# Bias rows of the gates as a pair of float32r rows instead of one float32 row, in a two-layer block on one core

## The chip, the cores and the metric

The kernel runs on one core of a Trainium2 chip. The metric is the device time of one execution in microseconds (us). Three executions of the kernel before took 2523.35, 2525.79 and 2533.22 us; their median is 2525.79 us.

## The reference

The program is a hybrid attention layer on 256 tokens of width 2048, followed by a recurrent layer with a convolutional feed-forward part. The change touches one product of the first layer, the projection that makes the gates:

```python
proj = jnp.einsum('bsd,dc->bsc', hn, w_in)                # hn: 256 x 2048
gates = jax.nn.sigmoid(proj[..., QKVG_COLS + N_HEADS:] + b_gate).reshape(b, s, N_BRANCH, D_MODEL)
# each branch's output is multiplied by its gate, and the three are summed
merged = sum over n of gates[:, :, n] * (y[n] @ w_up[n])  # 256 x 2048
```

`b_gate` has 3 x 2048 entries. The kernel treats it as twelve pieces of 512, one for each block of 512 gate columns.

## The kernel before

**Products.** Every large product takes its weights through four slots of 2 x 512 columns. For each such unit SyncE (SP) loads `w_raw`, ScalarE (ACT) writes its rounded part `w_hi` in float32r (L502), VectorE (DVE) writes the remainder `w_lo` (L839), and TensorE (PE) runs twelve matmuls (L1408): two chunks, two token tiles, and three terms (hi x hi, hi x lo, lo x hi). The semaphores `hi_done`, `lo_done` and `used` count units. ACT and DVE run two units ahead of PE; SP runs four ahead of DVE. The order on each engine is written out by hand, and each engine works strictly down its own list.

**Gate blocks.** Blocks 12 to 15 (`seg == 3`) are the gates of branch 0: eight units each, in alternating PSUM banks. ACT evacuates each with a sigmoid into `xn` (L581). Four short products with `w_up` follow; DVE multiplies each by its gate into `merged` (L1012).

**Pairs.** Then a hardware loop of four rounds, each with two halves (`j`), goes through eight pairs: a gate product of eight units in PSUM bank 0, and an up product of two units in bank 1. ACT turns the gate into `sg` by a sigmoid (L590). When the up product is done, DVE multiplies it by `sg` (L1021) and adds it to `merged` (L1023). PE does not wait for these two: its next gate product needs bank 0 alone, and that has been evacuated (`evac_act`). After the second half of a round DVE also copies a row of another product, the modulation (`mod_copy`, L957). Modulation units (L1435, two matmuls of 32 output rows) are woven between the units of the large products: `every_other`.

**Bias.** The bias enters PSUM ahead of a gate product, as a matmul with one row: `add_row` multiplies a one-row constant of ones by `brow`, once for each token tile.

```python
def add_row(bank):                                             # L1421 to L1423
    for rt in range(RT):
        pe.matmul(gemm_ps[:, bank, rt], C("sel", 1, 0, P), brow[:, :], start=True, stop=False)
```

SP fetches `brow` (L370, L380) when the gate product before has used the old one, and PE waits for that load (`brow_in`).

Of the kernel before, what the change touches and what calls it, by code (L numbers as in the profile page):

```python
# [4 lines left out]
F32 = mybir.dt.float32  # L22
F32R = mybir.dt.float32r
# [6 lines left out]
P = 128  # L30
T = 256
RT = T // P
D = 2048
# [132 lines left out]
def build(nc, a):  # L166
    base = (nc.sbuf_base + 31) // 32 * 32

    def at(name, shape, dtype, kb):
        return nc.alloc_sbuf_tensor_at(name, shape, dtype, offset=base + int(kb * KB))  # L170
# [15 lines left out]
    br = [at(f"br{i}", [P, RT, 4 * BW], F32, 129.5 + 16 * i) for i in range(2)]  # L186
    ys_hi = at("ys_hi", [P, NBR * HEADS, T], F32R, 161.5)
    ys_lo = at("ys_lo", [P, NBR * HEADS, T], F32R, 173.5)
    brow = at("brow", [1, NBLK], F32, 185.5)
    relb = at("relb", [P, HEADS, T], F32, 189.5)  # L190
    tmpT = at("tmpT", [P, 2, UK, T], F32, 193.5)
    sg = at("sg", [P, RT, NBLK], F32, 193.5)
# [91 lines left out]
    def S(name):  # L284
        if name not in sems:
            sems[name] = nc.alloc_semaphore(name)
        return sems[name]

    raw_in = [S(f"raw_in{i}") for i in range(SLOTS)]
    brow_in = S("brow_in")  # L290
    mod_in = [S(f"mod_in{i}") for i in range(SLOTS)]
    mod_used, mod_evac, mod_out = S("mod_used"), S("mod_evac"), S("mod_out")
    tr_use = {"x": 0, "merged": 1, "ctx": 2, "x1": 3, "y": 4, "x2": 5}
# [16 lines left out]
    with nc.Block() as block:  # L310
# [3 lines left out]
        def _(sp):  # L314
# [51 lines left out]
            bg = a["b_gate"]  # L366
            for g in range(DC):
                if g:
                    sp.wait_ge(used, U_GATE0 + BU * (g - 1) + 1)
                sp.dma_start(brow[:, :], bg[:, g * NBLK:(g + 1) * NBLK]).then_inc(brow_in, 16)  # L370
                b = 12 + g
                units(w_in, 2 * b, GATE0 + g * NBLK, mod=every_other(b // 2, b % 2))
            for c in range(DC):
# [2 lines left out]
            with sp.Fori(0, DC) as c:  # L376
                for j in range(2):

                    sp.wait_ge(used, U_PAIRS + 2 * PAIR * c + (1 if j else 1 - PAIR))
                    sp.dma_start(brow[:, :], bg[:, bass.ds((j + 1) * D + c * NBLK, NBLK)]).then_inc(brow_in, 16)  # L380
                    q = U_PAIRS // SLOTS + 2 * PAIR // SLOTS * c
                    units(w_in, q, GATE0 + (j + 1) * D + c * NBLK, PAIR * j, mod=every_other(8 + c, j))
                    units(w_up, q, c * NBLK, PAIR * j + BU, UPU, row=4 * (j + 1))
# [104 lines left out]
        def _(act):  # L488
# [15 lines left out]
            def splits(q, lo, hi, ffn=False):  # L504
                for i in range(lo, hi):
                    split(q + i // SLOTS, i % SLOTS, ffn)
# [49 lines left out]
            def forget_gates(B, i):  # L556

                if (B, i) == (2, 6):
# [2 lines left out]
                    me(act.activation(fl[:, 3:5, 0:HEADS], fl[:, 3:5, 0:HEADS], ACT.Exp, scale=-1.0))  # L561
                    act.activation(fl[:, 3:5, 0:HEADS], fl[:, 3:5, 0:HEADS], ACT.Ln, bias=1.0).then_inc(S("f_sp"), 1)

            for seg in range(4):
                for b in range(4):
                    B = 4 * seg + b
                    for i in range(2, 10):

                        if B == 0:
                            turned("x", i - 2)  # L570
                        splits(2 * B, i, i + 1)
                        if seg:
                            head(seg - 1, b, i)
                        else:
                            forget_gates(B, i)
                    act.wait_ge(used, BU * (B + 1))
                    if seg < 3:
                        act.activation(br[seg % 2][:, :, b * BW:(b + 1) * BW], gemm_ps[:, B % 2],
                                       ACT.Silu if b == 3 else ACT.Copy).then_inc(evac_act, 1)
                    else:  # L580
                        act.activation(xn[:, :, b * NBLK:(b + 1) * NBLK], gemm_ps[:, B % 2],  # L581
                                       ACT.Sigmoid).then_inc(evac_act, 1)
            splits(U_UP0 // SLOTS, 2, UPU * DC + 2)
            with act.Fori(0, DC) as c:
                q = U_PAIRS // SLOTS + 2 * PAIR // SLOTS * c
                for j in range(2):
                    splits(q, PAIR * j + 2, PAIR * j + BU + 2)
                    act.wait_ge(used, U_PAIRS + 2 * PAIR * c + PAIR * j + BU)
                    act.wait_ge(evac_dve, DC + 2 * c + j)
                    act.activation(sg[:], gemm_ps[:, 0], ACT.Sigmoid).then_inc(evac_act, 1)  # L590
                    splits(q, PAIR * j + BU + 2, PAIR * j + PAIR + 2)
# [241 lines left out]
        def _(dve):  # L833
# [7 lines left out]
            def splits(q, lo, hi):  # L841
                for i in range(lo, hi):
                    split(q + i // SLOTS, i % SLOTS)
# [130 lines left out]
            diagonals()  # L974
            splits(0, 0, 2)

            def forget_gates(B, i):
                if (B, i) == (2, 3):
                    dve.wait_ge(S("f_parts"), 1)
                    dve.tensor_copy(fparts[:, :], pC[:, 0:T]).then_inc(S("f_copied"), 1)  # L980
                if (B, i) == (2, 5):
                    dve.wait_ge(S("f_ps"), 1)
                    dve.tensor_tensor(fl[:, 1:3, 0:HEADS], pC[:, T:T + 64].rearrange("p (r h) -> p r h", r=RT)[:, :, 0:HEADS],
                                      fl[:, 0:1, 0:HEADS].to_broadcast([P, RT, HEADS]), ALU.add).then_inc(S("f_val"), 1)
                if (B, i) == (2, 8):
                    dve.wait_ge(S("f_sp"), 1)
                    dve.scalar_tensor_tensor(out=fl[:, 5:7, 0:HEADS], in0=fl[:, 1:3, 0:HEADS], scalar=0.0,
                                             in1=fl[:, 3:5, 0:HEADS], op0=ALU.min, op1=ALU.subtract).then_inc(S("f_log"), 1)
                if (B, i) == (3, 5):
                    dve.wait_ge(S("f_c"), 1)  # L990
                    dve.tensor_copy(cneg[0:HEADS, :], pC[0:HEADS, 0:T]).then_inc(S("f_cneg"), 1)

            for seg in range(4):
                for b in range(4):
                    B = 4 * seg + b
                    for i in range(2, 10):
                        if B == 0:
                            turned("x", i - 2, vec[:, 0:16])
                            turned_rest("x", i - 2)
                        splits(2 * B, i, i + 1)  # L1000
                        if seg:
                            head(seg - 1, b, i)
                        else:
                            forget_gates(B, i)
                    if B % 2:
                        mod_copy(B // 2)
# [7 lines left out]
            with dve.Fori(0, DC) as c:  # L1014
                me.iteration(first, 2 * c)
                q = U_PAIRS // SLOTS + 2 * PAIR // SLOTS * c
                for j in range(2):
                    splits(q, PAIR * j + 2, PAIR * j + PAIR + 2)
                    dve.wait_ge(evac_act, 16 + 2 * c + j + 1)
                    dve.wait_ge(used, U_PAIRS + 2 * PAIR * c + PAIR * (j + 1))  # L1020
                    me(dve.tensor_tensor(sg[:], gemm_ps[:, 1], sg[:], ALU.mult))  # L1021
                    m = merged[:, :, bass.ds(c * NBLK, NBLK)]
                    dve.tensor_tensor(m, m, sg[:], ALU.add).then_inc(evac_dve, 1)  # L1023
                mod_copy(8 + c)
# [359 lines left out]
        def _(pe):  # L1384
# [35 lines left out]

            def add_row(bank):  # L1421
                for rt in range(RT):
                    pe.matmul(gemm_ps[:, bank, rt], C("sel", 1, 0, P), brow[:, :], start=True, stop=False)  # L1423

            def mod_unit(m, i):

# [144 lines left out]
            for seg in range(4):  # L1571
                for b in range(4):
                    B = 4 * seg + b
                    if B >= 2:
                        pe.wait_ge(evac_act, B - 1)
                    if seg == 3:
                        pe.wait_ge(brow_in, 16 * (b + 1))
                        add_row(B % 2)

                    def after(u):  # L1580
                        if seg:
                            head(seg - 1, b, u)
                        else:
                            forget_gates(B, u)
                        every_other(B // 2, B % 2, u)
                    product(BU * B, 0, B % 2, a_hi, a_lo, BU, opened=(seg == 3), after=after,
                            turning=("x", x_sb, True, 0) if B == 0 else None)
# [9 lines left out]
            with pe.Fori(0, DC) as c:  # L1597
                for j in range(2):
                    u0 = U_PAIRS + 2 * PAIR * c + PAIR * j
                    pe.wait_ge(brow_in, 16 * (DC + 2 * c + j + 1))  # L1600
                    pe.wait_ge(evac_act, 16 + 2 * c + j)
                    add_row(0)
                    product(u0, PAIR * j, 0, a_hi, a_lo, BU, opened=True, after=lambda u: every_other(8 + c, j, u))
                    pe.wait_ge(evac_dve, DC + 2 * c + j)
                    product(u0 + BU, PAIR * j + BU, 1, ys_hi, ys_lo, UPU, chunk0=4 * (j + 1))
# [368 lines left out]
```

## Time and profile before

| | |
|---|---|
| median of three executions | 2525.79 us |
| their range | 2523.35 to 2533.22 us |
| profiled execution, first to last instruction | 2527.4 us |
| PE busy | 2443.7 us, 97% |
| DVE busy | 1397.4 us, 55% |
| ACT busy | 1046.0 us, 41% |
| mean granted TensorE clock | 0.984 of full speed |

The page gives no time for the profiled execution other than its span, which lies inside the range of the three. In the timeline a row is one instruction or several merged ones: start, duration, engine, line, operation, output from inputs, shape, count, and in brackets the idle time of the engine ahead of it with what ended it. Matmul ends are modelled and overlap the next start, so the distance between two starts is the pace. A float32 matmul leaves two records. PEclk is the clock granted to TensorE: 1.00 is 2.4 GHz and 0.50 is 1.2 GHz.

### The profile page before, as it was taken

How to read it: one execution, taken by the hardware profiler on the slowest of the kernel's cores; microseconds unless marked ns; L12 is line 12 of the kernel's file. 1: busy time of each engine (PE TensorE's matmuls, PEld its weight loads, DVE VectorE, ACT ScalarE, POOL GpSimd, SP SyncE). 2: the span in 40 equal slices, each digit the busy share in tenths (PEclk: the TensorE clock that was granted, in tenths of full speed). 3: DMA queues.
4: the chain of work that ended last, by engine and by line, in shares of the span. 5: the costliest groups of instructions: out<-in, count | busy, mean ns of one | idle time of the engine just before them, and what ended most of it. 6: DMA issues, size and time to landing. Idle time of an engine off the chain costs nothing.

```text
span 2527.4 us, 30821 instructions
## 1 busy us (share of the span) xinstructions
PE 2443.7 (97%) x10984; PEld 1818.5 (72%) x10984; DVE 1397.4 (55%) x2057; ACT 1046.0 (41%) x1304; POOL 77.4 (3%) x149
## 2 busy tenths in 40 slices
PE   6999999999999999999999999898999999999997
PEld 5677776676666676567578777665888888887886
DVE  4355553344443563344355577854677778785554
ACT  3333435433333433333743344432455555554432
POOL 0000000000000200000000000010000000000000
PEclk9999999999999999999999999999999999999999
DMA  7766666556666858886444333367555665566564
GB/s 237 234 223 205 206 201 197 185 193 215 217 204 217 285 193 283 264 261 217 149 126 117 117 89 87 92 206 241 166 172 186 191 191 177 180 195 201 182 201 138
DMA packets 297375, 482.72 MB, mean 191 GB/s; under 512 B 23075, under 2 KB 114405, under 8 KB 295089
## 3 DMA queue, kind: packets, MB, share of 16 engines
q1 hardware_dynamic: 290824, 464.85, 57.4%
q0 software_dynamic: 6448, 16.48, 1.9%
q8 instruction: 67, 1.10, 0.2%
q14 instruction: 36, 0.29, 0.0%
HBM read 474.56 MB, written 6.69 MB: 190 GB/s over the span
## 4 chain that ended last, share of the span: by engine, by line
PE 88%; DVE 5%; ACT 3%; issue 2%; DMA 1%; SPq 0%; DVEq 0%; POOL 0%; ACTq 0%
PE gemm_ps L1408 71%; PE ps L1435 7%; ACT w_hi L502 1%; PE gemm_ps L1423 1%; PE ps L1764 1%; DVE w_lo L839 1%; PE ps L1460 1%; PE ps L1817 1%; PE ps L1904 1%; PE ps L1824 1%; DVE tmpT L870 1%; PE ps L1769 0%; PE ps L1471 0%; DMA w_raw<-in_w_down_dram 0%; DVE sc L1270 0%
## 5 line engine op out<-in xcount | busy, mean ns | idle before, releaser
L839 DVE TENSOR_TENSOR w_lo<-w_raw,w_hi 128x1024 fp32r<-128x1024 f32 x688 | 832.7, 1223 | 771.6 <-ACT w_hi L502 765.7
L502 ACT ACTIVATE w_hi<-w_raw 128x1024 fp32r<-128x1024 f32 x688 | 716.6, 1054 | 627.4 <-PE gemm_ps L1408 486.7
L1408 PE MATMUL gemm_ps<-w_hi,a_hi 128*128 128x512 f32 (+1 forms) x2304 | 953.5, 414 | 14.9 <-DVE a_lo L877 13.9
L1408 PE MATMUL gemm_ps<-w_hi,a_lo 128*128 128x512 f32 (+1 forms) x2304 | 903.7, 392 | 0.0
L1408 PE MATMUL gemm_ps<-w_lo,a_hi 128*128 128x512 f32 (+1 forms) x2304 | 903.5, 392 | 0.0
L1408 PEld LDWEIGHTS gemm_ps<-w_hi,a_hi 128*128 128x128 f32 x2304 | 437.8, 190 | 270.6 <-issue 141.9
L1408 PEld LDWEIGHTS gemm_ps<-w_hi,a_lo 128*128 128x128 f32 x2304 | 437.5, 190 | 95.6
L1408 PEld LDWEIGHTS gemm_ps<-w_lo,a_hi 128*128 128x128 f32 x2304 | 438.5, 190 | 88.4 <-issue 8.4
L1435 PE MATMUL ps<-mraw,cs 128*32 128x512 f32 x768 | 202.3, 605 | 3.3 <-DMA mraw<-in_w_mod_dram 2.9
L1327 DVE SCALAR_TENSOR_TENSOR acc<-gp,cw,acc 128x256 f32<-128x256 f32 x344 | 151.5, 480 | 13.8 <-DVE acc L1327 1.4
L1408 PE MATMUL gemm_ps<-w_hi,ft_hi 128*128 128x512 f32 x344 | 135.9, 395 | 2.3 <-DVE w_lo L839 2.3
L1408 PE MATMUL gemm_ps<-w_lo,ft_hi 128*128 128x512 f32 x344 | 135.1, 393 | 0.0
L1408 PE MATMUL gemm_ps<-w_hi,ft_lo 128*128 128x512 f32 x344 | 135.0, 393 | 0.0
L431 POOL DMA_DIRECT2D mod_d<-mrow x96 | 50.0, 521 | 1306.6 <-DVE mrow L957 1302.3
L512 ACT ACTIVATE a_hi<-tmpT 128x512 fp32r<-128x512 f32 x48 | 30.3, 632 | 138.5 <-DVE tmpT L870 115.5
L1408 PEld LDWEIGHTS gemm_ps<-w_hi,ft_hi 128*128 128x128 f32 x344 | 65.5, 190 | 17.7 <-issue 4.0
L1408 PEld LDWEIGHTS gemm_ps<-w_lo,ft_hi 128*128 128x128 f32 x344 | 65.6, 191 | 13.6
L1408 PEld LDWEIGHTS gemm_ps<-w_hi,ft_lo 128*128 128x128 f32 x344 | 65.3, 190 | 13.7
L1435 PEld LDWEIGHTS ps<-mraw,cs 128*32 128x32 f32 x768 | 28.1, 108 | 61.1 <-issue 53.6
L799 ACT ACTIVATE ub<-gemm_ps 128x1024 f32<-128x1024 f32 x22 | 22.6, 1028 | 90.4 <-PE gemm_ps L1408 90.4
L877 DVE TENSOR_TENSOR a_lo<-tmpT,a_hi 128x512 fp32r<-128x512 f32 x48 | 33.2, 692 | 36.4 <-ACT a_hi L512 36.4
L870 DVE TENSOR_SCALAR tmpT<-ps,vec 128x256 f32<-128x256 f32 x80 | 37.8, 513 | 23.9 <-PE ps L1460 23.0
(344 smaller groups left out, 1560.2 us busy)
## 6 DMA issues: line engine op xcount, KB each, us to landing
w_raw<-in_w_in_dram SPq DMA_DIRECT2D x336, 512.0 KB, 4.0
mraw<-in_w_mod_dram SPq DMA_DIRECT2D x192, 512.0 KB, 4.9
w_raw<-in_w_up_dram SPq DMA_DIRECT2D x336, 256.0 KB, 3.2
w_raw<-in_w_down_dram SPq DMA_DIRECT2D x84, 512.0 KB, 4.2
w_raw<-in_w_out_dram SPq DMA_DIRECT2D x64, 512.0 KB, 4.8
w_raw<-in_w_up_dram SPq DMA_DIRECT2D x24, 512.0 KB, 4.8
x_d<-xres POOLq DMA_DIRECT2D x2, 2048.0 KB, 8.0
x_sb<-in_x_dram SPq DMA_DIRECT2D x2, 1024.0 KB, 6.0
```

The source lines that it names most:

```text
L431: pool.dma_start(mod_d[g, :, bass.ds(m * NBLK, NBLK)], mrow[32 * g:32 * g + 2, :]).then_inc(mod_out, 16)
L502: act.activation(w_hi[:, slot], raw[:, slot], ACT.Copy).then_inc(hi_done, 1)
L512: act.activation(a_hi[:, UK * g:UK * g + UK], tmpT[:, g % 2], ACT.Copy).then_inc(S("tr_hi"), 1)
L839: dve.tensor_tensor(w_lo[:, slot], raw[:, slot], w_hi[:, slot].bitcast(F32), ALU.subtract).then_inc(lo_done, 1)
L870: ins = dve.tensor_scalar(tmpT[:, g % 2, k], bank[:, k * T:(k + 1) * T], scale[:, kc:kc + 1], b, ALU.mult, ALU.add if bias is not None els ...
L877: dve.tensor_tensor(a_lo[:, UK * g:UK * g + UK], tmpT[:, g % 2], a_hi[:, UK * g:UK * g + UK].bitcast(F32), ALU.subtract).then_inc(S("tr_lo ...
L1327: ins = dve.scalar_tensor_tensor(out=a_f, in0=gp[:, f, dy:dy + 4, dx:dx + 64], scalar=cw[:, bass.ds(tap * FCH + (b - 1) * 2 + f, 1)], in1=a_f,
L1408: mm = pe.matmul(gemm_ps[:, bank, rt, 0:n], x[:, chunk0 + k, tok], w[:, slot, kk, 0:n], start=(k == 0 and part == 0 and not opened), stop= ...
L1423: pe.matmul(gemm_ps[:, bank, rt], C("sel", 1, 0, P), brow[:, :], start=True, stop=False)
L1435: mm = pe.matmul(pD[32 * g:32 * g + 32, :], cs[:, k], mraw[:, i % SLOTS, kk], start=(k < 4), stop=(k >= KC - 4), skip_group_check=True)
L1460: mm = pe.matmul(out, part, diag[:, rt], start=True, stop=True)
L1764: pe.matmul(numb[d][:, rt * GDV:(rt + 1) * GDV], mpT[:, at0:at0 + P], v[t][:, h * GDV:(h + 1) * GDV], start=(n == 0), stop=(n == len(seen) ...
```

## The change

`bsrc` receives the bias piece twice, in two partitions. ACT multiplies the two copies by +1 and -1 and writes them rounded to float32r into the two rows of `brow`. DVE then adds the unrounded bias to the second row alone, so that row 0 holds the rounded bias and row 1 the remainder. `ones2` is a float32r tile of ones with two rows, and the matmul of `add_row` sums the two rows in PSUM. PE now waits for DVE's step (`brow_set`) and no longer for the load; SP fetches the next piece after DVE's step as well. The column of +1 and -1 and the ones are made once, in block 3.

```diff
-    brow = at("brow", [1, NBLK], F32, 185.5)
+    bsrc = at("bsrc", [2, NBLK], F32, 185.5)
+    brow = at("brow", [2, NBLK], F32R, 187.5)
+    ones2 = at("ones2", [2, P], F32R, 204)
...
# SP, blocks 12 to 15
-                    sp.wait_ge(used, U_GATE0 + BU * (g - 1) + 1)
-                sp.dma_start(brow[:, :], bg[:, g * NBLK:(g + 1) * NBLK]).then_inc(brow_in, 16)
+                    sp.wait_ge(brow_set, g)
+                sp.dma_start(bsrc[:, :], bg[0, g * NBLK:(g + 1) * NBLK].partition_broadcast(2)).then_inc(brow_in, 16)
...
# SP, pairs
-                    sp.wait_ge(used, U_PAIRS + 2 * PAIR * c + (1 if j else 1 - PAIR))
-                    sp.dma_start(brow[:, :], bg[:, bass.ds((j + 1) * D + c * NBLK, NBLK)]).then_inc(brow_in, 16)
+                    sp.wait_ge(brow_set, DC + 2 * c + j)
+                    sp.dma_start(bsrc[:, :], bg[0, bass.ds((j + 1) * D + c * NBLK, NBLK)].partition_broadcast(2)).then_inc(brow_in, 16)
...
# ACT
+            def bias_row(n, row_used):
+                act.wait_ge(S("ones_set"), 1)
+                act.wait_ge(brow_in, 16 * (n + 1))
+                act.wait_ge(used, row_used)
+                act.activation(brow[:, :], bsrc[:, :], ACT.Identity, scale=stat[0:2, 46:47]).then_inc(brow_hi, 1)
...
+                    if seg == 3:
+                        bias_row(b, U_GATE0 + BU * (b - 1) + 1)
...
                 for j in range(2):
+                    bias_row(DC + 2 * c + j, U_PAIRS + 2 * PAIR * c + (1 if j else 1 - PAIR))
                     splits(q, PAIR * j + 2, PAIR * j + BU + 2)
...
# DVE
+            def bias_row(n):
+                dve.wait_ge(brow_hi, n + 1)
+                dve.scalar_tensor_tensor(out=brow[:, :], in0=bsrc[:, :], scalar=ident[0:2, 1:2], in1=brow[:, :].bitcast(F32),
+                                         op0=ALU.mult, op1=ALU.add).then_inc(brow_set, 1)
...
+                if (B, i) == (3, 8):
+                    dve.memset(ones2[:, :].bitcast(F32), 1.0)
+                    dve.tensor_tensor(stat[0:2, 46:47], ident[0:2, 0:1], ident[0:2, 1:2], ALU.subtract).then_inc(S("ones_set"), 1)
...
+                    if seg == 3:
+                        bias_row(b)
...
                 for j in range(2):
+                    bias_row(DC + 2 * c + j)
                     splits(q, PAIR * j + 2, PAIR * j + PAIR + 2)
...
# PE
-                    pe.matmul(gemm_ps[:, bank, rt], C("sel", 1, 0, P), brow[:, :], start=True, stop=False)
+                    pe.matmul(gemm_ps[:, bank, rt], ones2[:, :], brow[:, :], start=True, stop=False)
...
-                        pe.wait_ge(brow_in, 16 * (b + 1))
+                        pe.wait_ge(brow_set, b + 1)
...
-                    pe.wait_ge(brow_in, 16 * (DC + 2 * c + j + 1))
+                    pe.wait_ge(brow_set, DC + 2 * c + j + 1)
```

The first place is DVE's list at the end of a pair's first half, in the loop over the pairs. `sg<-gemm_ps,sg` is the product with the gate, `br<-br,sg` the sum into `merged`, and `w_lo` the remainders of the weights. ISA and REGISTER_ALU rows are waits and counts. Before:

```order
L839 TENSOR_TENSOR w_lo<-w_raw,w_hi 128x1024
L1019 ISA
L1020 ISA
L1021 TENSOR_TENSOR sg<-gemm_ps,sg 128x1024
L158 REGISTER_ALU
L1023 ISA
L1023 TENSOR_TENSOR br_61<-br_61,sg 128x2x512
L838 ISA
L839 TENSOR_TENSOR w_lo<-w_raw,w_hi 128x1024
```

With the change:

```order
L835 TENSOR_TENSOR w_lo<-w_raw,w_hi 128x1024
L1027 REGISTER_ALU
L1028 ISA
L1029 TENSOR_TENSOR sg<-gemm_ps,sg 128x1024
L142 REGISTER_ALU
L1031 ISA
L1031 TENSOR_TENSOR br_61<-br_61,sg 128x2x512
L975 REGISTER_ALU
L976 SCALAR_TENSOR_TENSOR brow<-bsrc,cst,brow 2x512
L834 ISA
L835 TENSOR_TENSOR w_lo<-w_raw,w_hi 128x1024
```

The step that writes the bias row stands behind both operations of the pair before. The line numbers in the changed kernel differ by a few.

The second place is ACT's list between two of the blocks 12 to 15, with the change; `xn<-gemm_ps` is the evacuation of the block before. Without the L555 row it is the list of before, table load included:

```order
L528 ACTIVATE ys_hi<-yT 128x256
L576 ACT_TABLE_LOAD
L576 ACTIVATE xn<-gemm_ps 128x2x512
L555 ACTIVATE brow<-bsrc,stat 2x512
L488 ACTIVATE w_hi<-w_raw 128x1024 x3
L507 ACTIVATE qkgT<-ps 128x256
```

The rounding of the next bias row stands behind that evacuation.

## Rows read from the trace of the kernel before

**Rows 1.** The page: busy time (part 1) and the chain that ended last (part 4).

```profile
PE 2443.7 (97%) x10984; PEld 1818.5 (72%) x10984; DVE 1397.4 (55%) x2057; ACT 1046.0 (41%) x1304; POOL 77.4 (3%) x149
...
PE 88%; DVE 5%; ACT 3%; issue 2%; DMA 1%; SPq 0%; DVEq 0%; POOL 0%; ACTq 0%
```

**Rows 2.** Groups by line, L1423: busy us, mean ns | idle before, its releaser.

```profile
L1423 PE MATMUL gemm_ps<-brow,cst 1*128 1x512 f32 x48 | 25.2, 647 | 1.6 <-DVE br L1012 1.6
```

**Rows 3.** Stretches of time: engines' busy time, then granted clock, DMA share, GB/s.

```profile
454.40:457.80 3.40, 3.40 (x10) 2.57 (x10) 1.28 (x2) 0.00 (x0) 1.40 (x3) 0.52 0.59 174
543.10:549.90 6.80, 6.80 (x13) 3.62 (x13) 1.71 (x2) 0.00 (x0) 0.00 (x0) 0.51 0.87 300
550.00:819.00 269.00, 269.00 (x1107) 184.42 (x1106) 112.55 (x95) 89.01 (x86) 6.23 (x12) 1.00 0.65 209
```

**Rows 4.** Timeline of PE and DVE where the sixth pair follows the fifth.

```profile
716.11 0.39 PE L1408 MATMUL gemm_ps<-w_hi,ys_lo 128*128 128x512 f32 x1
...
716.79 0.39 PE L1408 MATMUL gemm_ps<-w_hi,ys_lo 128*128 128x512 f32 x1
717.11 1.98 PE L1423 MATMUL gemm_ps<-brow,cst 1*128 1x512 f32 x4
...
717.22 1.22 DVE L1021 TENSOR_TENSOR sg<-gemm_ps,sg 128x1024 f32<-128x1024 f32 x1 [2.21 <-PE gemm_ps L1408]
718.59 1.23 DVE L1023 TENSOR_TENSOR br<-br,sg 128x1024 f32 x1
719.02 0.50 PE L1408 MATMUL gemm_ps<-w_hi,a_hi 128*128 128x512 f32 x1
719.36 0.39 PE L1408 MATMUL gemm_ps<-w_lo,a_hi 128*128 128x512 f32 x1
...
719.73 1.22 DVE L839 TENSOR_TENSOR w_lo<-w_raw,w_hi 128x1024 fp32r<-128x1024 f32 x1
```

**Rows 5.** Timeline, next boundary, where a new round begins: PE, then DVE.

```profile
750.99 0.39 PE L1408 MATMUL gemm_ps<-w_hi,ys_lo 128*128 128x512 f32 x1
...
753.81 0.69 DVE L957 COPY mrow<-ps 128x512 f32<-128x512 f32 x1
754.41 2.35 DVE L839 TENSOR_TENSOR w_lo<-w_raw,w_hi 128x1024 fp32r<-128x1024 f32 x2
```

**Rows 6.** Groups by line and shape: the nearest to the added operations.

```profile
L1148 DVE SCALAR_TENSOR_TENSOR la<-ps,spd 128x512 f32<-128x512 f32 x4 | 2.7, 682 | 0.0
...
L512 ACT ACTIVATE a_hi<-tmpT 128x512 fp32r<-128x512 f32 x48 | 30.3, 632 | 138.5 <-DVE tmpT L870 115.5 <-DVE tmpT L865 23.0
```

**Rows 7.** Timeline after the last pair, where PE waits for `merged`.

```profile
821.05 1.22 DVE L1023 TENSOR_TENSOR br<-br,sg 128x1024 f32 x1
...
822.38 1.20 PE L1462 MATMUL ps<-cst,br 128*128 128x128 f32 x8 [2.62 <-DVE br L1023]
```

**Rows 8.** Timeline where block 13 follows block 12: PE and ACT.

```profile
419.45 1.02 ACT L581 ACTIVATE xn<-gemm_ps 128x1024 f32<-128x1024 f32 x1 [0.57 <-PE gemm_ps L1408]
420.33 1.98 PE L1423 MATMUL gemm_ps<-brow,cst 1*128 1x512 f32 x4
420.37 1.99 ACT L502 ACTIVATE w_hi<-w_raw 128x1024 fp32r<-128x1024 f32 x2
...
422.57 0.39 PE L1408 MATMUL gemm_ps<-w_lo,a_hi 128*128 128x512 f32 x1
```

**Rows 9.** Timeline ahead of the first pair: DVE and PE.

```profile
541.32 1.22 DVE L1012 TENSOR_TENSOR br<-gemm_ps,xn 128x1024 f32<-128x1024 f32 x1 [1.95 <-PE gemm_ps L1408]
...
542.46 2.35 DVE L839 TENSOR_TENSOR w_lo<-w_raw,w_hi 128x1024 fp32r<-128x1024 f32 x2
542.90 3.44 PE L1423 MATMUL gemm_ps<-brow,cst 1*128 1x512 f32 x4 [1.62 <-DVE br L1012]
...
546.27 0.80 PE L1408 MATMUL gemm_ps<-w_hi,a_hi 128*128 128x512 f32 x1
```

**Rows 10.** SP's queue: a bias load in the pairs.

```profile
660.00 0.25 SPq L380 DMA_DIRECT2D brow<-in_b_gate_dram  x1
```

More of the change, by code:

```diff
@@ L289, in build @@
     raw_in = [S(f"raw_in{i}") for i in range(SLOTS)]
-    brow_in = S("brow_in")
+    brow_in, brow_hi, brow_set = S("brow_in"), S("brow_hi"), S("brow_set")
     mod_in = [S(f"mod_in{i}") for i in range(SLOTS)]
```

## The prediction

> **What bounds the kernel.** I read the page first. PE is busy for 97% of the span and holds 88% of the chain that ended last [rows 1]. So what counts is how long PE's own list takes, and what PE waits for. The second view is the changed line: it shows 48 records of 647 ns on average, two for each of 24 matmuls, and one wait, of 1.6 us [rows 2]. The third is the table of stretches. From 550 to 819 us, most of the pair loop, PE is busy for all of 269.00 us at a clock of 1.00 [rows 3]: it waits for nobody, and no other engine's work is on its path. Any time taken off PE there is a gain in full, and any wait put there is a loss in full. The last view is the timeline at three kinds of boundaries where a bias row is written, because the change moves the release of PE.
>
> **The row itself.** A float32r matmul starts every 0.227 us (716.11 to 716.79 are three) [rows 4]. From the last up matmul at 716.79 to the second gate matmul at 719.36 PE needs 2.57 us, with two float32 matmuls in between [rows 4]. As two float32r matmuls they make four intervals of 0.227, or 0.91 us. That saves 1.66 us for each bias row, and 12 x 1.66 = 19.9 us in all, if PE never waits. Two partitions instead of one change nothing that I can see in the rows; the bounds for a bias matmul in float32r are 0.227 us and, if two rows of depth should cost what one float32 row did, 0.95 us (1.91 / 2, 717.11 to 719.02 [rows 4]). I take the lower one, since the type is that of the 0.227 us rows.
>
> **The new wait in the pairs (seven boundaries).** PE now starts the row when DVE has written it, and DVE's list has that step behind both operations of the pair before. These begin only when the up product has ended: 717.22 and 718.59, and DVE is free at 719.73 [rows 4]. ACT's half is early: its step stands ahead of splits that wait for PE, and it needs only a landed load and the first unit of the pair before. DVE's step is a scalar_tensor_tensor of 512 columns; the nearest row took 0.68 us [rows 6]. The way from DVE to PE lies between two measured ones: 822.38 - 821.05 - 1.22 = 0.11 us [rows 7] and 542.90 - 541.32 - 1.22 = 0.36 us [rows 9]. With their middle, PE starts the row at 719.73 + 0.68 + 0.24 = 720.65 instead of at 716.79 + 0.23 = 717.02. That is a wait of 3.6 us against a saving of 1.66: **+2.0 us** at each of the four boundaries inside a round. Between rounds DVE also copies the modulation row first and is free at 754.41; PE starts at 755.33 instead of 751.22, a wait of 4.1 us [rows 5], or **+2.45 us**, three times. Together 4 x 2.0 + 3 x 2.45 = 15.4 us. With either way to PE for all seven: 14.5 to 16.3.
>
> **The clock.** While PE idles, the granted clock can fall. After a wait of 1.62 us, PE's first records at 542.90 and on ran at half speed [rows 9], and the clock stood at 0.51 until 549.9, which is the 1.2 GHz level [rows 3]. A shorter stretch at that level is 454.4 to 457.8 [rows 3]. In the pair loop there is none now [rows 3]; with seven waits of 3.6 to 4.1 us, longer than the one at 541, I expect one behind most of them. Ends: nothing, and a stretch of 6.8 us worked at half speed, which loses some 3.2 us, so 0 to 22 us. I take a short stretch (3.4 us) of which a third falls into the wait and the rest is worked at half speed: 1.15 us each, **+8 us**, by the row at 454.4, since PE works densely again behind each wait. The Trainium skill, "TensorE: Matmul & The Clock Gate", section "HAM oscillation", has the same pattern: a loop whose matmul bursts are parted by waits pays the transition at each of them. By that rule the sum has this term for every boundary; without it the sum would be 8 us smaller. The rows at 541 are on the rule's side, and no row here shows a series of such waits.
>
> **The first pair.** PE already waits for DVE here, 1.62 us, until 542.90, and DVE is free at 542.46 [rows 9]. PE now starts at 542.46 + 0.92 = 543.38, at the low clock; two float32r matmuls take 0.9 us there, and the gate begins at 544.3 instead of 546.27: -2.0. If the low stretch then ends one short stretch earlier (546.5), another 1.6 us is saved; I take **-2.7 us** between -2.0 and -3.6.
>
> **Blocks 12 to 15.** ACT's half of the row stands behind its evacuation of the block before, so nothing is early here. At 420.37 ACT is free of the evacuation that began at 419.45 [rows 8]. The rounding of 512 columns takes 0.63 us and DVE's step 0.68 [rows 6]; with 0.24 to PE, the row starts at 421.95 instead of 420.33: a wait of 1.6 us. From the row's start to the second gate matmul it was 2.24 us [rows 8] and will be 3 x 0.227 = 0.68, which saves 1.56. So each of the four comes out even, +0.1 us; **+0.4 us**. The modulation copy that DVE makes ahead of two of them lasts as long as ACT's step and lies beside it. No table load is added on ACT.
>
> **Costed at nothing.** The load of the piece now has two rows and goes out after `brow_set` of the row before. SP issued the one at 660.00 some 23 us ahead of its use [rows 10], while it waited for slots, and the step it now waits for lies a whole pair further back. If this cover were gone, PE would wait for the landing of a small load at each row. ACT's and DVE's added steps (12 x 0.63 and 12 x 0.68 us) lie on engines that are busy for 41% and 55% [rows 1]; DVE resumes its splits 0.7 us later, but PE has two finished units ahead of it, more than 5 us of work. The ones and the signs are two short steps of DVE, once.
>
> **Sum.** 15.4 + 8.0 - 2.7 + 0.4 = +21 us on a profiled span of 2527.4, which is 1.6 us above the median of the runs. On the median: 2525.8 + 21 = 2547. Later low-clock stretches will shift against the work, and I round to **2547.5 us**, 0.86% slower. About 0.5% is what a measurement of this kernel can tell from no change, here 13 us.
>
> **Rivals.**
> 1. *The clock holds.* Row intervals are as I say, but no wait drops the clock: +13 us, 2539. For it: bias rows of 1.9 us in the pairs do not drop it now. Against: the rows at 541. Chance 0.15.
> 2. *The clock falls for long.* Each wait leaves a stretch like 543.1 to 549.9 [rows 3]: 7 x 3 = 21 instead of 8, 2560. For: that stretch follows the nearest wait. Against: there a slow float32 row kept PE on light work for another 3.4 us [rows 9]. Chance 0.13.
> 3. *Faster.* DVE writes the row beside the up product. If the step came before the two operations of the pair before, its operand would be ready and all 19.9 us would be kept except at blocks 12 to 15, where 1.6 us each is waited: about -14 us, 2512. It decides at one point: whether the step starts before the up product has ended (717.0). DVE's list speaks against it. Chance 0.03.
> 4. *The row is not cheaper.* A float32r matmul of two rows takes 0.95 us: nothing is saved, and the waits remain: 21 + 12 x 1.45 = +38 us, 2564. Against: every float32r row at L1408. Chance 0.03.
> 5. *The load is late.* SP stands at `brow_set` and weights come late behind it. Some 2 us a boundary more, 2563. Against: rows 10. Chance 0.03.
>
> **How the numbers follow.** My forecast has 0.63 and a spread of its own, 2541 to 2554, from 14.5 to 16.3 for the waits, from 3 to 14 for the clock, and from where stretches at the low clock fall elsewhere. The range takes in rival 1 and most of rival 2: 2537 to 2558. Over 0.5% slower starts at 2538.4: the forecast and rivals 2, 4 and 5 lie there, and rival 1 half: 0.87. Within 0.5%: half of rival 1 and a little of the forecast, 0.10. Faster: 0.03.
>
> **What would show it.** In the profile after, the 24 bias matmuls should have one record each of about 0.39 us, 0.23 us apart. PE should have seven waits of 3.3 to 4.2 us ahead of them, put down to DVE's step, and ACT's step should be done long before. In blocks 12 to 15 the waits should be about 1 to 2 us. From 550 to 835 the clock should show stretches at 0.5 behind most of the waits. The forecast is wrong if the waits in the pairs are under 2 us, if the bias matmuls stand 0.4 us or more apart at full clock, or if the clock stays at 1.00 there.

## The result, and the profile after

The changed kernel took 2557.86 us (median of four executions, 2555.54 to 2561.81) against 2529.51 us (median of four as well, 2523.35 to 2533.35) for the kernel before: a ratio of 1.0112, with a 95% interval of 1.0098 to 1.0127. It is slower by some 28 us. The profiled execution took 2557.57 us, with a span of 2555.9 us, 28.5 more than the span before.

The first view is the page's busy time:

```profile
PE 2438.0 (95%) x10960; PEld 1820.4 (71%) x10960; DVE 1406.1 (55%) x2071; ACT 1053.4 (41%) x1316; POOL 77.7 (3%) x149
```

PE has 24 records less than in [rows 1], since each of the 24 bias matmuls now leaves one, and it is busy for 95% instead of 97%. It has no more work than before; it waits. The groups by line of the new operations (busy us, mean ns of one, idle time ahead and what ended it):

```profile
L1431 PE MATMUL gemm_ps<-brow,ones 2*128 2x512 f32 x24 | 9.9, 493 | 33.8 <-DVE brow L976 33.8
...
L976 DVE SCALAR_TENSOR_TENSOR brow<-bsrc,cst,brow 2x512 fp32r<-2x512 f32 x12 | 8.8, 734 | 6.1 <-ACT brow L555 6.1
L555 ACT ACTIVATE brow<-bsrc,stat 2x512 fp32r<-2x512 f32 x12 | 8.5, 706 | 0.0
```

The bias matmuls take 9.9 us instead of 25.2, and PE stands idle ahead of them for 33.8 us instead of 1.6 [rows 2]. The timeline at the same boundary as in [rows 4], the sixth pair after the fifth, shows what ends a wait:

```profile
735.09 0.39 PE L1416 MATMUL gemm_ps<-w_hi,ys_lo 128*128 128x512 f32 x1
...
735.52 1.23 DVE L1029 TENSOR_TENSOR sg<-gemm_ps,sg 128x1024 f32<-128x1024 f32 x1 [2.21 <-PE gemm_ps L1416]
736.88 1.22 DVE L1031 TENSOR_TENSOR br<-br,sg 128x1024 f32 x1
738.03 0.73 DVE L976 SCALAR_TENSOR_TENSOR brow<-bsrc,cst,brow 2x512 fp32r<-2x512 f32 x1
...
738.89 1.21 PE L1431 MATMUL gemm_ps<-brow,ones 2*128 2x512 f32 x2 [3.41 <-DVE brow L976]
740.03 0.80 PE L1416 MATMUL gemm_ps<-w_hi,a_hi 128*128 128x512 f32 x1
740.62 0.63 PE L1416 MATMUL gemm_ps<-w_lo,a_hi 128*128 128x512 f32 x1
```

The row starts 3.80 us after the last up matmul, where I had forecast 3.86. From 739 on PE runs at half speed: its matmuls are 0.59 us apart instead of 0.34 [rows 4]. Where a new round begins, DVE copies the modulation row first and the wait is longer:

```profile
778.93 0.72 PE L1431 MATMUL gemm_ps<-brow,ones 2*128 2x512 f32 x2 [3.90 <-DVE brow L976]
```

The table of stretches for blocks 12 to 15, for the pairs, and for one stretch behind a wait (PE's busy time stands first, the granted clock third from the right):

```profile
387.00:520.00 133.00, 126.60 (x551) 90.36 (x549) 51.22 (x57) 70.53 (x84) 4.17 (x8) 0.96 0.56 179
550.00:817.00 267.00, 241.63 (x961) 168.32 (x959) 105.42 (x94) 83.97 (x84) 6.25 (x12) 0.95 0.62 193
...
739.20:745.80 6.60, 6.60 (x16) 4.72 (x16) 1.83 (x2) 0.24 (x1) 0.00 (x0) 0.51 0.69 217
```

In the pairs PE was busy all the time at a clock of 1.00 [rows 3]. Now it misses 25 us of 267, and the clock is 0.95.

**The account.** I compared the starts of the same matmuls of the large products in both timelines. The changed kernel is 1.5 us late at 387 us, before the first bias row: for an early load PE waits 5.33 us instead of 2.93, and this wait comes and goes between executions (3.12 us in a later run that has the same work there). Blocks 12 to 15 and the four up products behind them add 3.1 us. The first pair gives back 2.55 us at its row, and 1.5 more in the stretch that ran at half speed before [rows 3]. From there to the second gate matmul of the eighth pair the shift grows by 30.0 us. Another 1.15 comes behind this last row, where the clock falls once more, and 3.25 is given back later, where other stretches at the low clock happen to fall. Together 1.5 + 3.1 - 4.05 + 30.0 + 1.15 - 3.25, some 28.5 us.

### The profile page after: what moved, and what is told of

Same layout as the page of the kernel before. It is cut to its first block, busy times and chain, and to the rows that moved or that the text cites. A ratio compares the mean times of both kernels' runs of the same rounds, so it can differ in the third digit from the quotient of the medians.

```text
span 2555.9 us, 30831 instructions
## 1 busy us (share of the span) xinstructions
PE 2438.0 (95%) x10960; PEld 1820.4 (71%) x10960; DVE 1406.1 (55%) x2071; ACT 1053.4 (41%) x1316; POOL 77.7 (3%) x149
## 4 chain that ended last, share of the span: by engine, by line
PE 87%; DVE 5%; ACT 3%; issue 2%; DMA 1%; SPq 0%; DVEq 0%; POOL 0%; ACTq 0%
PE gemm_ps L1416 70%; PE ps L1443 7%; ACT w_hi L488 1%; PE ps L1772 1%; DVE w_lo L835 1%; PE ps L1825 1%; PE ps L1468 1%; PE ps L1912 1%; PE ps L1832 1%; DVE tmpT L866 1%; PE ps L1777 0%; PE ps L1479 0%; DMA w_raw<-in_w_down_dram 0%; DVE sc L1278 0%; DVE sg L1029 0%
## 5 line engine op out<-in xcount | busy, mean ns | idle before, releaser
L1416 PE MATMUL gemm_ps<-w_hi,a_hi 128*128 128x512 f32 (+1 forms) x2304 | 957.8, 416 | 15.4 <-DVE a_lo L873 14.4
```

What stands on the lines that cost most here:

```text
L1416: mm = pe.matmul(gemm_ps[:, bank, rt, 0:n], x[:, chunk0 + k, tok], w[:, slot, kk, 0:n], start=(k == 0 and part == 0 and not opened), stop= ...
```

## The experiments

Two theories stood against each other. One says that the place of DVE's step is the loss: PE waits for two operations that it never waited for, and the clock falls behind the waits. The other says that the new row, the added steps or the load cost time themselves. The last row of the table is for reference.

| run | median, us | before beside it, us | ratio (95%) |
|---|---|---|---|
| rows early in the pairs | 2522.67 | 2530.20 | 0.9974 (0.9963 to 0.9986) |
| all rows early | 2508.29 | 2530.20 | 0.9920 (0.9903 to 0.9937) |
| only the wait | 2567.62 | 2530.20 | 1.0155 (1.0135 to 1.0174) |
| row between the two operations | 2544.46 | 2530.20 | 1.0062 (1.0038 to 1.0086) |
| waits filled | 2547.16 | 2531.29 | 1.0066 (1.0048 to 1.0083) |
| no rows | 2500.50 | 2531.29 | 0.9879 (0.9862 to 0.9895) |
| all early, 128 partitions | 2507.00 | 2531.29 | 0.9911 (0.9895 to 0.9928) |
| the same, first pair too | 2505.62 | 2531.29 | 0.9904 (0.9887 to 0.9920) |
| the change | 2557.86 | 2529.51 | 1.0112 (1.0098 to 1.0127) |

**Rows early in the pairs.**

```diff
# DVE, pairs; ACT and SP go one row ahead in the same way
+            bias_row(DC)
             with dve.Fori(0, DC) as c:
...
-                    bias_row(DC + 2 * c + j)
                     splits(q, PAIR * j + 2, PAIR * j + PAIR + 2)
+                    bias_row(DC + 2 * c + j + 1)
                     dve.wait_ge(evac_act, 16 + 2 * c + j + 1)
```

> The changed kernel, but in the pairs DVE writes the next bias row ahead of its product with the gate, as soon as ACT has rounded it; the row of the first pair is written before the loop. The last round writes one row that nobody uses. Theory (place of DVE's step): the seven waits of 3.3 to 3.9 us and the low-clock stretches behind them are gone, the clock from 550 to 850 us is 1.00, and each of these rows costs PE 0.9 us from the last up matmul to the second gate matmul instead of 2.57 before. Against before: 7 x -1.66 for the pairs, -2.6 for the first pair, +1.6 for blocks 12 to 15: about -12.6 us (0.995). Rival (the float32r row of two partitions, the added steps or the load cost time themselves): it stays slower than before by 5 us or more.

It came out faster than before, at 0.9974. All seven waits in the pairs are gone, and of 33.8 us of waiting 8.4 is left, at the first five rows. So the place of DVE's step was the loss, and the rival falls. But the gain is smaller than expected: each row in the pairs gives 1.25 us and not 1.66, 8.9 us in all instead of 11.6, and blocks 12 to 15, where PE still waits and the clock is 0.96 as in the changed kernel, cost 3.1 us instead of 1.6.

**All rows early.**

```diff
# ACT, ahead of the evacuation; the same on DVE, ahead of mod_copy
+                    if 11 <= B < 15:
+                        bias_row(B - 11, U_GATE0 + BU * (B - 12) + 1)
                     act.wait_ge(used, BU * (B + 1))
```

> As the run with early rows in the pairs, and in blocks 12 to 15 as well: ACT rounds and DVE writes the next row before ACT evacuates the block and before DVE copies the modulation row. Theory: PE waits at no bias row except before the first pair, and the four rows save 1.56 us each as well: about -20 us against before (0.992). Rival (there ACT's or DVE's extra step delays the evacuation or the splits): the four rows save nothing, -12 us, with new waits of PE for ACT's evacuation.

The size came out as expected, 0.992. PE waits at one row only, the first pair's, for 2.1 us. The stretch of blocks 12 to 15, first of the kernel before, then of this run (columns as above):

```profile
387.00:520.00 133.00, 133.00 (x570) 92.37 (x569) 49.37 (x55) 69.93 (x83) 4.16 (x8) 0.97 0.55 179
```

```profile
387.00:520.00 133.00, 133.00 (x599) 95.52 (x598) 57.16 (x64) 77.22 (x91) 6.23 (x12) 1.00 0.58 190
```

The clock went from 0.97 to 1.00. The sum is right for a reason that I had left out: each row saves less than I said (below), and the stretches at the low clock in these blocks, as the one at 454.4 in [rows 3], are gone. At the first pair the clock still fell, from 537.2 to 540.6 us. The rows of a boundary between two pairs:

```profile
702.24 0.39 PE L1420 MATMUL gemm_ps<-w_hi,ys_lo 128*128 128x512 f32 x1
...
702.55 0.73 PE L1435 MATMUL gemm_ps<-brow,ones 2*128 2x512 f32 x2
...
703.55 0.40 PE L1420 MATMUL gemm_ps<-w_lo,a_hi 128*128 128x512 f32 x1
```

From the last up matmul to the second gate matmul it takes 1.31 us, four intervals of 0.33, where I had counted 0.227.

**Only the wait.**

```diff
                     pe.wait_ge(evac_act, 16 + 2 * c + j)
+                    pe.wait_ge(evac_dve, DC + 2 * c + j)
                     add_row(0)
...
-                    pe.wait_ge(evac_dve, DC + 2 * c + j)
```

> The kernel before, with its float32 rows, but PE's wait for DVE's sum of the pair before (which it makes anyway ahead of the up product) is moved ahead of the bias row. Nothing is added, only the wait. Theory (the wait and the clock are the loss): seven waits of 2.6 to 2.9 us and a stretch at the 1.2 GHz level behind nearly each, 7 x (2.9 + 1.6) = +31 us against before (1.012), as much as the change. Rival (the new rows and steps are the loss): +20 us or less with the clock at 1.00, or under +5 us if the wait is absorbed.

One moved wait, with the float32 rows as they were and no added step, makes the kernel slower by 1.55%: more than the change itself. Its waits are shorter than the change's:

```profile
PE gemm_ps L1423 <- DVE br L1023: 18.9, 7, 2.8
```

That is 18.9 us in seven waits, the longest 2.8. The shift grows by 33.9 us from the first to the eighth pair, so some 15 of it is not waiting. The clock from 550 to 817 us is 0.94. The row behind a wait still runs at full clock, the whole of it in four of the seven cases and its first half or more in the others:

```profile
740.03 1.95 PE L1423 MATMUL gemm_ps<-brow,cst 1*128 1x512 f32 x4 [2.78 <-DVE br L1023]
```

Without a wait it took 1.98 us [rows 4]. The gate product behind it is what runs slowly: behind four of the seven rows for 3.4 us, behind three for 6.8, while in the changed kernel two of the seven stretches are that long.

**Row between the two operations.**

```diff
                     me(dve.tensor_tensor(sg[:], gemm_ps[:, 1], sg[:], ALU.mult))
+                    bias_row(DC + 2 * c + j + 1)
```

> As the run with early rows in the pairs, but DVE's step stands between the product with the gate and the sum. PE waits for one of DVE's long operations instead of two (and a copy): the row starts about 2.6 us after the last up matmul instead of 3.8 to 4.3. Without a loss of clock each of seven boundaries costs 2.6 + 0.9 - 2.57 = +0.9 us: with the first pair and blocks 12 to 15 some +5 us against before. Theory A (the clock falls behind shorter waits too): another 1 to 1.5 us each, +12 to +16 us. Theory B (the clock falls only behind the long ones): +5 us, the clock at 1.00 from 550 to 835 us.

The waits in the pairs were 2.3 us at most, and each boundary cost +1.07 us. The shift also grew by 1.6 us inside four of the pairs, where the clock fell: in the stretch from 550 to 817 us it is 0.97. So theory A holds for four of the seven boundaries, and theory B for the other three; the total, +14 us, lies in theory A's range. Waits of this size cost clock behind some of the boundaries, those of 3.4 to 3.9 us in the changed kernel behind all.

**Waits filled.**

```diff
+                    for _ in range(14):
+                        pe.matmul(pA[:, :], a_hi[:, 0, 0:P], a_hi[:, 0:2].rearrange("p a b -> p (a b)"), start=True, stop=True)
                     pe.wait_ge(brow_set, DC + 2 * c + j + 1)
```

> The changed kernel with work for PE in its waits: ahead of each wait for the bias row in the pairs, 14 float32r matmuls of 128x512 (3.2 us at full clock) that write a PSUM bank nobody reads. Every wait for DVE is as before, only the idle time is filled. Theory (the clock is a loss of its own, some 11 us of the change's loss in the pairs): the clock from 550 to 830 us is 1.00, and each of the seven boundaries costs 2.2 to 2.8 us against before. At the first pair the filler itself costs about 2.4 us, since PE hardly waits there. So against the changed kernel -11 + 2.4, about +20 us against before (1.008). Rival (the low-clock stretches come from something else, such as the kind of matmul that follows, or cost nothing): the time is that of the changed kernel plus 2.4 us, +30 us (1.012).

The same boundary with the filler, and the stretch of the pairs:

```profile
729.84 3.33 PE L1609 MATMUL ps<-a_hi 128*128 128x512 f32 x14
...
733.41 0.71 PE L1431 MATMUL gemm_ps<-brow,ones 2*128 2x512 f32 x2 [0.24 <-DVE brow L976]
```

```profile
550.00:817.00 267.00, 263.84 (x1109) 186.87 (x1108) 109.82 (x96) 86.11 (x86) 6.22 (x12) 1.00 0.62 201
```

The row still waits for DVE's step, but PE is busy for most of that time, and the clock stays at 1.00. The seven boundaries cost 2.2 us inside a round and 2.7 between rounds, which is what they cost in the changed kernel when the slow stretches are left out. From the end of the first pair to the end of the eighth the shift grows by 17.1 us instead of 31.2: keeping PE busy takes 14.1 us off the change's loss in the pairs, 1.6 us behind five of the waits and 3.1 behind the two with the long stretches. At the first pair the filler costs 2.8 us, 0.4 more than expected: PE starts it only when DVE's last product with `w_up` is done, so it fills no more than the last 0.6 us of the wait. Useless work that keeps PE busy makes the changed kernel some 11 us faster (2547 against 2558; the two ran beside different executions of the kernel before, with ratios of 1.0066 and 1.0112).

**No rows.**

```diff
-                        add_row(B % 2)
...
-                    add_row(0)
```

> The kernel before without its bias matmuls: the bias is left out of the gates, its loads stay. This measures the floor of what the row can give. From the last up matmul to the second gate matmul PE needs two intervals, 0.46 us instead of 2.57: 12 x 2.1 = 25 us less, and 2 to 3 us more where stretches at the low clock in blocks 12 to 15 and at the first pair go: -28 us (0.989). The run with all rows early then holds about 20 of the 28. Rival: something else than PE's list bounds one of these stages (loads, ACT), and it gains no more than the run with all rows early, -20 us.

This kernel leaves the bias out, so it does not compute the layer; it gives a floor. The floor is 0.9879, or -31 us, where I had expected 28. So all early float32r rows hold some 20 of 31 us.

**All early, 128 partitions.**

```diff
-    brow = at("brow", [2, NBLK], F32R, 187.5)
-    ones2 = at("ones2", [2, P], F32R, 204)
+    brow = at("brow", [P, NBLK], F32R, 187.5)
+    ones2 = at("ones2", [P, P], F32R, 204)
...
+                    me(dve.memset(brow[:, :].bitcast(F32), 0.0))
+                    me(dve.memset(ones2[:, :].bitcast(F32), 0.0))
+                    dve.memset(ones2[0:2, :].bitcast(F32), 1.0)
```

> As the run with all rows early, but the two operands of the bias matmul have 128 partitions, of which 126 hold zeros. In that run a float32r bias matmul of two partitions stood 0.33 us after its predecessor where the others stand 0.23 apart. Theory A (changing the number of partitions between neighbouring matmuls costs some 0.1 us per matmul, since the weights' load is then not hidden): the intervals are 0.23, each row costs PE 0.91 us instead of 1.31, and the run is 12 x 0.4 = 5 us faster than the one with all rows early, about -25 us against before. Theory B (the depth has no part in it): the intervals stay 0.33 and the time stays -20 us against before.

Theory A's intervals are there:

```profile
696.06 0.39 PE L1422 MATMUL gemm_ps<-w_hi,ys_lo 128*128 128x512 f32 x1
696.28 0.62 PE L1437 MATMUL gemm_ps<-brow,ones 128*128 128x512 f32 x2
...
696.97 0.39 PE L1422 MATMUL gemm_ps<-w_lo,a_hi 128*128 128x512 f32 x1
```

0.91 us instead of 1.31, so each row in the pairs saves 1.66 against [rows 4]. In blocks 12 to 15, where a modulation unit stands ahead of the row, it is less than the expected 0.4 us: 1.32 us instead of 1.51 from that unit's last record to the second gate matmul. The weight loads (PEld) of the row bear out the reason that theory A gives, first with two partitions (the run with all rows early), then with 128:

```profile
702.55 0.29 PEld L1435 LDWEIGHTS gemm_ps<-brow,ones 2*128 2x128 f32 x2 [0.35 <-issue]
```

```profile
696.06 0.41 PEld L1437 LDWEIGHTS gemm_ps<-brow,ones 128*128 128x128 f32 x2
```

With two partitions the load starts together with the row's own matmul (702.55); with 128 it starts 0.22 us ahead of it (696.28), beside the matmul before. In the time it is not settled: -24 us against before, but the intervals of this run's ratio and of the two-partition run's overlap. The trace shows it, the medians can't.

**The same, first pair too.**

```diff
# DVE: bias_row(DC) ahead of the last product with w_up; PE:
-            pe.wait_ge(evac_dve, DC)
+            pe.wait_ge(evac_dve, DC - 1)
```

> As the run with bias matmuls of 128 partitions, and the row of the first pair is written ahead of DVE's last product with w_up, while PE enters the pairs when the bank that it writes is free instead of waiting for that product. Expected: PE's wait of 2.1 us at the first pair goes, and the stretch at the low clock behind it; 2.4 + 1.6 = 4 us less than that run, about -29 us against before (0.989) if theory A of that run holds, -24 if B does. Rival: PE runs into a wait for the next unit's weights there, which ACT and DVE have not split yet, and gains less than 1 us.

PE no longer waits at any bias row, and at the first pair the second gate matmul follows the last up matmul after 0.91 us instead of 3.23 in the run before this one: 2.3 us less. The 1.6 us of clock that I had counted on top were not there to gain: the clock stood at 1.00 from 380 to 550 us in both. The low stretch that I had read (537.2 to 540.6) stands in the run with all rows early, and not in the one before this. The time, 0.9904, can't be told from that run's 0.9911. Both beat the kernel before by about 1%, and the changed kernel by about 2%.

## Why the prediction was right

The forecast was 2547.5 us within 2537 to 2558, slower with a chance of 0.87. The measured 2557.86 lies 0.14 us inside the upper end, and the change is +28 us where the sum said +21. The mechanism was the forecast one: new waits of PE for DVE's step, and low-clock stretches behind them. That the time fell inside the range is in part luck, since the four executions lie 6 us apart; and 3.7 us of the distance come from the kernel before, whose median was 2525.79 us when I forecast and 2529.51 beside the change. In the profiled executions the terms came out 1.7 us higher for the waits, 6.1 for the clock and 2.7 for blocks 12 to 15, and 1.4 lower for the first pair. Two to which I had given no number, 1.5 us at an early load and -3.25 for later stretches at the low clock, take part of that back.

- **The new wait in the pairs** held: seven waits put down to DVE's step, 3.41 and 3.90 us in the two boundaries shown. The row starts within 0.1 us of what DVE's list and its durations gave. Its cost was 2.2 us inside a round and 2.7 between rounds (2.0 and 2.45 forecast), 17.1 us in all instead of 15.4, because the row saves less.
- **The row itself** was the first mis-sized term. I wrote that two partitions "change nothing that I can see in the rows", and took 0.227 us per matmul. It is 0.33 with two partitions, so a row in the pairs saves 1.25 us where PE does not wait, and not 1.66. The run with 128 partitions shows that the number of partitions is the cause. Where PE waits, the first of the four intervals lies in the wait, and the other three make 0.3 us at each of the seven boundaries and of blocks 12 to 15: about 3.4 us of the change's loss. I had the bound (0.95 us), and took the lower end without asking what the change of shape costs next to full matmuls.
- **The clock** was the second, and the larger: 8 us forecast, 14.1 measured by filling the waits. Each boundary costs 2.0 us of clock on average, and not 1.15. I took a short stretch of which a third falls into the wait. In the trace of the changed kernel no more than 0.1 us of any stretch does, so a short one costs 1.6 us, and two were nearly 7 us long, as the one at 739.2 to 745.8, and cost 3.1. The Trainium skill's pattern ("TensorE: Matmul & The Clock Gate", section "HAM oscillation": each burst behind a wait pays the transition again) is borne out by the changed kernel's trace at all seven boundaries.
- **The first pair** gave 4.05 us and not 2.7: no low stretch followed the row at all, the case that I had put at the far end (3.6). The shorter row is not enough for that. With all rows early PE waited the same 2.05 us ahead of the same row, and the clock fell from 537.2 to 540.6 us. What decides it stays open.
- **Blocks 12 to 15** were forecast even, +0.4. PE waited 1.60 us at each, as forecast, but with the smaller saving each row cost 0.4 us, and the clock fell behind three rows where it had fallen behind two, another 1.6: 3.1 us together.
- **Costed at nothing** held for the load and for the steps on ACT and DVE: with all rows early, the same loads and steps stand there and the kernel is 20 us faster than before.
- Of the **rivals**, the clock that holds is excluded; the clock that falls for long is true at two of the seven boundaries, and the measured +28 us lies halfway between my +21 and its +34. The rival on the other side named the right point: when the step starts before the up product has ended, the sign turns, and two runs show it, at 0.9974 and 0.992.

## What to carry to other kernels

When an operand gets an extra preparation step, ask what stands ahead of that step on the list of the engine that makes it. A step of 0.7 us queued behind two operations that nobody waited for made the engine that bounds the kernel wait for all three; moved ahead of them, the same step cost it no wait. And on an engine that is the bound, price a recurring wait with the clock that it costs: here seven waits, 25 us in all, cost another 14 us through the half-speed work behind them.

## What the runs showed of the hardware

A float32r matmul of two partitions between neighbours of 128 costs more than its columns: the intervals around it were 0.33 us, against 0.227 us when the same matmul was padded with zeros to 128 partitions. A float32 matmul of one row cost 0.95 us [rows 4]. Padding gave 0.4 us a row in the pairs for two operations of DVE that write the zeros once, 0.49 and 0.17 us; whether the whole time is shorter by it, the medians can't tell.

The granted clock fell to the 1.2 GHz level behind four of seven waits of 2.3 us, behind all seven of 3.4 to 3.9 us, and, at the first pair, behind one of five waits of 2.05 us for the float32r row. In blocks 12 to 15 it fell even in the kernel before, behind two of the four rows (454.4 to 457.8 [rows 3], and 488.7 to 492.1), with PE busy throughout: what it did just before was a modulation unit of 32 output rows and a float32 bias row. In these executions neither of the two did it alone. In the pairs of the kernel before seven float32 rows stand behind full matmuls, and the clock stayed at 1.00; in the run without rows the modulation units of blocks 12 to 15 are still there, and from 387 to 520 us it stayed at 1.00, too. With the rows early and in float32r the clock did not fall there either.
